# Four window products in adjoining slots: a denser slot table in the attention stage of a decoder layer

## The chip, the cores and the metric

The kernel runs on one core of one Trainium2 chip. The metric is the device time of one execution in microseconds. The engines are TensorE (PE: matmuls and transposes; its weight loads are listed apart as PEld), VectorE (DVE), ScalarE (ACT), GpSimd (POOL) and SyncE (SP), which here only issues DMAs. Each has its own in-order queue of instructions, and they meet at semaphores.

## The reference, cut to what matters

One layer of a decoder is computed for a prompt of 1024 tokens and for 8 samples of 4 new tokens each. The change touches the attention alone:

```python
DIL_CONFIGS = ((128, 1), (512, 4), (2048, 16))     # window, dilation; 8 heads x 64
# prompt: three dilated branches over its own k, v, combined by their softmax denominators
# sample: the same over the cached window (2048 rows of k and v) and the new rows
kc = jnp.concatenate([win_k, k], axis=1)
vc = jnp.concatenate([win_v, v], axis=1)
for _, dil in DIL_CONFIGS:
    o_i, l_i = dilated_branch_sample(q, kc, vc, dil)
attn = combine_branches(outs, lses)
```

Then follow a depthwise convolution module beside it, an output projection, cross-attention into 256 memory tokens and a gated FFN. The outputs are the new activations and the caches.

## The kernel before, in words

The three branches are one softmax with a bias that counts how many branches see a key. Of a sample's 2048 cached rows only 896 are seen by any branch: the last 512, and four in every sixteen of the older ones. Such a **window** is 7 tiles of 128 rows by 512 columns (1.8 MB), loaded by 4 DMAs (`window`, from L452). There are 16 of them, a key and a value window for each of 8 samples. They alternate between two buffers, `cached[0]` and `cached[1]`, in the order of `ORDER_W`: keys of samples 0 to 3, values of 0 to 3, keys of 4 to 7, values of 4 to 7. SP issues a window when the last reader of the one two places before it is done (L466 to L472); for a value window that reader is a **window product** (semaphore `spv`).

The stage is a loop over 34 **steps** (L1269). A prompt step s is one block i of 128 queries and one pair of heads. PE does, in step s: the scores of s (`scores`, in two parts from block 4 on), the product of probabilities and values of step s-2 (`product`), and the transposes of the probabilities of s-1 (`turn_p`, also in two parts). DVE adds the bias and takes the maxima (`maxima`, `negate`), ACT exponentiates (`probabilities`) and copies the transposes to SBUF (`turned`, tile `PT`).

The samples' attention is threaded through this loop in **slots**, three to a step from step 2 on. Slot number `r` of group `g` comes from `sample_slot` (L329): `divmod(3 * (s - 2) + pos, SAMPLE)`. There are two groups of four samples. In a group:

- slots 0 to 27: PE turns one key tile (`key_turn`), ACT or DVE copies it to `KTS` (ACT where the tile's number is divisible by 3, `on_scalar`), and in the next slot PE multiplies it with the queries (`key_scores`);
- slot 28 closes the scores; 29 and 30: bias and maximum on DVE, exponential on ACT; 32: normalisation of `Ps` on DVE; 33: PE transposes `Ps` (`turn_ps`); 34: ACT and DVE copy it to `PTS`;
- slots 35, 37, 39 and 41: the four window products (`window_product`), each 32 matmuls; slots 36, 38 and 40 are empty;
- slot 42: ACT copies the result to `OSs`; 43: PE turns it, and DVE copies it to `attsT`.

The order within a step is written out on each engine (L1269 to L1282 for PE, L1786 to L1799 for DVE, L674 to L688 for ACT). In PE's, the first slot stands behind the prompt product, the second behind the second part of the scores, the third at the end.

After the stage SP waits for the last prompt product (L474) and loads the memory rows (`mtk`), on whose norms PE's next matmuls depend.

Of the kernel before, what the change touches and what calls it, by code (L numbers as in the profile page):

```python
# [84 lines left out]
def pieces(c):  # L85

    out, g = [], c * CW
    while g < (c + 1) * CW:
        r = g % P
        n = min(P - r, (c + 1) * CW - g, (SEQ if g < SEQ else NTOK) - g)  # L90
        out.append((g // P, r, n, g - c * CW))
        g += n
    return out
# [11 lines left out]
class Signals:  # L105
# [14 lines left out]
    def mark(self, name, key, by=1):  # L120
        n = SHARED.get(name, name)
        self.now[n] = self.now.get(n, 0) + by
        assert (name, key) not in self.noted, (name, key)
        self.noted[name, key] = self.now[n]
        return self.sem(name), by
# [5 lines left out]
def layout(nc, ctx, A, O, counts):  # L131
# [183 lines left out]
    STEPS = [(i, hp) for i in range(TT) for hp in range(AT)]  # L315
    NP = len(STEPS)
    GROUP = 4 * KTILES
    SAMPLE = 44
    ORDER_W = [(kind, b) for g in range(2) for kind in "kv" for b in range(4 * g, 4 * g + 4)]
    STEP_W0 = 2  # L320
    LAST_STEP = max(NP + 1, STEP_W0 + 2 * SAMPLE // 3)

# [6 lines left out]
    def sample_slot(s, pos):  # L329
        g, r = divmod(3 * (s - STEP_W0) + pos, SAMPLE)  # L330
        return (g, r) if s >= STEP_W0 and g < 2 else (0, -1)

    def window_of(kind, b):
        n = ORDER_W.index((kind, b))
        return n, n % 2

    def on_scalar(n):
        return n % 3 == 0
# [211 lines left out]
    def _(act):  # L550
# [81 lines left out]
        def sample(g, r):  # L632

            if 0 <= r < GROUP and on_scalar(g * GROUP + r):
                n = g * GROUP + r
                act.wait_ge(*at("ktr", n))
                if n >= 2:
                    act.wait_ge(*at("ssc", n - 2))
                act.activation(KTS[n % 2][:, :, :], bank[5][:, :].rearrange("p (k n) -> p k n", k=AT), ACT.Copy).then_inc(*mark("ktsa", n))  # L639
            if r == GROUP + 2:  # L640
                act.wait_ge(*at("smax", g))
                act.activation(Ps[:, :], Ps[:, :], ACT.Exp, bias=negm[:, 2:3], accum_out=den[:, 2:3]).then_inc(*mark("sexp", g))
            if r == GROUP + 6:
                act.wait_ge(*at("sptr", g))
                if g:
                    act.wait_ge(*at("spv", 3))
                act.activation(PTS[:, 4:7, :], bank[7][:, 0:384].rearrange("p (a n) -> p a n", n=P), ACT.Copy).then_inc(*mark("spta", (g, 0)))
                act.activation(PTS[0:NS, KTILES, :], bank[7][0:NS, 384:512], ACT.Copy).then_inc(*mark("spta", (g, 1)))
            if r == GROUP + 14:
                act.wait_ge(*at("spv", 4 * g + 3))  # L650
                if g:
                    act.wait_ge(*at("sot", 0))
                else:
                    act.wait_ge(*at("cst_out", BD - 1))
                act.activation(OSs[:, :], bank[5][:, :], ACT.Copy).then_inc(*mark("os", g))
# [232 lines left out]
        for t in range(NX):  # L888
# [3 lines left out]
            g, even = divmod(t - HEAD0 - 1, 2)  # L892
# [144 lines left out]
        for g in range(2 * len(pieces(CH - 1))):  # L1037
            i, r, n, off = pieces(CH - 1)[g // 2]
# [16 lines left out]
    def _(pe):  # L1055
        reader = {}

        def take(b, name, key):

            if b in reader:  # L1060
                pe.wait_ge(*at(*reader[b]))
            reader[b] = (name, key)

        def turn(out, in_, r=0):
            n = in_.shape[0]
            return pe.transpose(out, in_, ident[r:r + n, r:r + n])  # L1066

        def mm(out, lhsT, rhs, first, last):
            return pe.matmul(out, lhsT, rhs, start=first, stop=last)  # L1069
# [162 lines left out]
        def window_product(b):  # L1232
            w, c = window_of("v", b)
            g = b // 4
            if b % 4 == 0:
                take(5, "os", g)
                pe.wait_ge(*at("spt", g))
                pe.wait_ge(*at("spta", (g, 1)))
            pe.wait_ge(*at(f"cached{c}", (w, OLD // P - 1)))
            cols = slice(P * (b % 4), P * (b % 4) + P)  # L1240
            for a in range(KTILES):
                for k in range(AT):
                    mm(bank[5][32 * k:32 * k + 32, cols], PTS[:, a, 32 * k:32 * k + 32], cached[c][:, a, k * P:(k + 1) * P], a == 0, False)
            for k in range(AT):
                ins = mm(bank[5][32 * k:32 * k + 32, cols], PTS[0:NS, KTILES, 32 * k:32 * k + 32], V[0:NS, TT, k * P:(k + 1) * P], False, True)
            ins.then_inc(*mark("spv", b))

        def sample(g, r):

            if r == 0:  # L1250
                group_scores(g)
            if 1 <= r <= GROUP:
                key_scores(g * GROUP + r - 1)
            if 0 <= r < GROUP:
                key_turn(g * GROUP + r)
            if r == GROUP:
                group_close(g)
            if r == GROUP + 5:
                turn_ps(g)
            if r - GROUP - 7 in (0, 2, 4, 6):  # L1260
                window_product(4 * g + (r - GROUP - 7) // 2)
            if r == GROUP + 15:
                take(5, "satt", (g, 3, 1))
                pe.wait_ge(*at("os", g))
                for b in range(4):
                    ins = turn(bank[5][:, b * P:(b + 1) * P], OSs[:, b * P:(b + 1) * P])
                ins.then_inc(*mark("sot", g))
# [320 lines left out]
        for g in range(2 * len(pieces(c))):  # L1588
            i, r, n, off = pieces(c)[g // 2]
# [8 lines left out]
    def _(dve):  # L1598
# [115 lines left out]
        def sample(g, r):  # L1714

            if 0 <= r < GROUP and not on_scalar(g * GROUP + r):
                n = g * GROUP + r
                dve.wait_ge(*at("ktr", n))
                if n >= 2:
                    dve.wait_ge(*at("ssc", n - 2))  # L1720
                dve.tensor_copy(KTS[n % 2][:, :, :], bank[5][:, :].rearrange("p (k n) -> p k n", k=AT)).then_inc(*mark("ktsd", n))
            if r == GROUP + 1:
                dve.wait_ge(*at("sall", g))
                if g:
                    dve.wait_ge(*at("sptr", g - 1))
                pieces_s = ((0, 512, bank[6][:, 0:512], ws[:, 0:512]), (512, KEYS, bank[7][:, 0:KEYS - 512], ws[:, 512:KEYS]),
                            (KEYS, KEYS + NS, bank[7][:, KEYS - 512:KEYS - 512 + NS], ws[:, KEYS + g * NS:KEYS + (g + 1) * NS]))
                for k, (k0, k1, src, bias) in enumerate(pieces_s):
                    if k:
                        dve.wait_ge(*at("sm", (g, k - 1)))  # L1730
                    masked_max(Ps[:, k0:k1], src, bias, mx[:, 0, k:k + 1], mx[:, 0, k - 1:k] if k else -3e38).then_inc(*mark("sm", (g, k)))
                dve.wait_ge(*at("sm", (g, 2)))
                dve.tensor_scalar(negm[:, 2:3], mx[:, 0, 2:3], -1.0, None, ALU.mult).then_inc(*mark("smax", g))
            if r == GROUP + 4:
                dve.wait_ge(*at("sexp", g))
                dve.reciprocal(rden[:, 2:3], den[:, 2:3]).then_inc(*mark("srd", g))
                dve.wait_ge(*at("srd", g))
                dve.tensor_scalar(Ps[:, :], Ps[:, :], rden[:, 2:3], None, ALU.mult).then_inc(*mark("spn", g))
            if r == GROUP + 6:
                dve.wait_ge(*at("sptr", g))  # L1740
                if g:
                    dve.wait_ge(*at("spv", 3))
                dve.tensor_copy(PTS[:, 0:4, :], bank[6][:, :].rearrange("p (a n) -> p a n", n=P)).then_inc(*mark("spt", g))
            if r == GROUP + 15:
                dve.wait_ge(*at("sot", g))
                for b in range(4):
                    v = bank[5][:, b * P:(b + 1) * P].rearrange("p (k y) -> p k y", y=32)
                    cols = slice((4 * g + b) * TD, (4 * g + b + 1) * TD)
                    for e in range(2):
                        rows = slice(64 * e, 64 * e + 64)  # L1750
                        dve.tensor_copy(attsT[rows, :, cols], v[rows, :, 8 * b + 4 * e:8 * b + 4 * e + 4]).then_inc(*mark("satt", (g, b, e)))
# [211 lines left out]
        for t in range(NX):  # L1963
            name, c, m = XU[t]
            g, odd = divmod(t - HEAD0 - 1, 2)
# [38 lines left out]
            g, odd = divmod(t - HEAD0, 2)  # L2004
# [78 lines left out]
        for g in range(2 * len(pieces(CH - 1))):  # L2083
            i, r, n, off = pieces(CH - 1)[g // 2]
# [42 lines left out]
```

## Time and profile before

| | |
|---|---|
| median of 3 runs | 1959.87 us (1957.81 to 1961.22) |
| the profiled execution | 1957.81 us, span 1955.7 us |
| PE busy | 1803.6 us, 92% of the span |
| DVE, ACT, POOL busy | 1018.8, 873.7, 834.1 us |
| mean granted clock of PE | 0.972 |
| DMA | 231.66 MB, mean 118 GB/s |

Busy time counts an engine's own work, not its waits. The span is that of the profiled core; the time of an execution is 2.1 us more. The attention stage reaches from about 316 to 569 us of the span.

### The profile page before, as it was taken

To read this page: it belongs to the slowest core of one execution; us is meant where nothing else is said; L and a number is where in the kernel's file an instruction comes from. 1 tells how busy PE (TensorE), PEld (TensorE's weight loads), DVE (VectorE), ACT (ScalarE), POOL (GpSimd) and SP (SyncE) were. 2 spreads that over 40 slices of the span, in tenths; PEclk is the share of its full clock that TensorE was granted. 3 is DMA by queue.
4 is the path that set the end of the run, shared out by engine and by line. 5 is a ranking of instruction groups with operands and counts; after the bars stand their busy time and mean duration, and the time that the engine had idled before them with its cause. 6 is when DMAs were issued, how large, how long until landed. Compare 5 with 4: busy or idle time off the path is not lost.

```text
span 1955.7 us, 30930 instructions
## 1 busy us (share of the span) xinstructions
PE 1803.6 (92%) x12222; PEld 1658.7 (85%) x12222; DVE 1018.8 (52%) x1749; ACT 873.7 (45%) x1663; POOL 834.1 (43%) x634
## 2 busy tenths in 40 slices
PE   3998997899968888789999988999999999999999
PEld 1898996567656778789887888999999999999998
DVE  3399992444425325773233567763148540388701
ACT  5211222344454545555544554554454543555533
POOL 1122231000002534454332445776667666677664
PEclk9999998999988889899999988999999999999999
DMA  5011223443212444444435333444444544444543
GB/s 170 22 46 41 88 82 115 140 163 114 80 57 65 121 135 124 116 142 154 129 115 171 93 93 101 140 133 137 134 137 140 151 143 137 138 138 140 150 135 105
DMA packets 348645, 231.66 MB, mean 118 GB/s; under 512 B 7915, under 2 KB 322401, under 8 KB 348495
## 3 DMA queue, kind: packets, MB, share of 16 engines
q1 hardware_dynamic: 342483, 218.19, 37.1%
q10 hardware_dynamic: 6020, 11.51, 1.6%
q8 instruction: 98, 1.61, 0.4%
q14 instruction: 44, 0.36, 0.1%
HBM read 218.58 MB, written 11.50 MB: 118 GB/s over the span
## 4 chain that ended last, share of the span: by engine, by line
PE 75%; DVE 14%; ACT 6%; issue 3%; DMA 2%; SPq 0%; ACTq 0%; POOL 0%; DVEq 0%
PE bank L1069 68%; PE bank L1066 7%; DVE C L1600 4%; DVE Y L1600 2%; DVE op_lo L1600 2%; DVE XT L1885 1%; DVE Sx L1873 1%; ACT whi L559 1%; ACT junk L572 1%; DVE cv L1600 1%; DVE carry L2043 1%; DVE Sy L1866 0%; SPq L413 0%; DVE op_x L1888 0%; ACT KTS L639 0%
## 5 line engine op out<-in xcount | busy, mean ns | idle before, releaser
L546 POOL TENSOR_TENSOR wlo<-raw,whi 128x512 fp32r<-128x512 f32 (+1 forms) x624 | 833.3, 1357 | 1103.3 <-ACT whi L559 1102.9
L1069 PE MATMUL bank<-op_hi,whi 128*128 128x352 f32 x1632 | 542.9, 333 | 10.2 <-ACT Y L810 8.7
L1069 PE MATMUL bank<-op_hi,wlo 128*128 128x352 f32 x1632 | 529.0, 324 | 0.0
L1069 PE MATMUL bank<-op_lo,whi 128*128 128x352 f32 x1632 | 528.3, 324 | 0.0
L559 ACT ACTIVATE whi<-raw 128x1024 fp32r<-128x1024 f32 (+1 forms) x312 | 325.1, 1043 | 303.8 <-PE bank L1069 84.2
L1069 PEld LDWEIGHTS bank<-op_hi,whi 128*128 128x128 f32 x1632 | 310.5, 190 | 20.0 <-ACT Y L810 9.9
L1069 PEld LDWEIGHTS bank<-op_lo,whi 128*128 128x128 f32 x1632 | 311.6, 191 | 0.3
L1069 PEld LDWEIGHTS bank<-op_hi,wlo 128*128 128x128 f32 x1632 | 310.1, 190 | 0.0
L1866 DVE TENSOR_TENSOR Sy<-Sy,SQy 128x352 f32<-128x352 f32 x63 | 40.2, 638 | 297.9 <-ACT SQy L772 297.9
L1600 DVE SCALAR_TENSOR_TENSOR C<-U,cw,C 128x1024 f32<-128x1024 f32 x120 | 176.5, 1471 | 4.0
L1069 PE MATMUL bank<-fhi,whi 128*128 128x352 f32 x528 | 171.1, 324 | 0.0
L1069 PE MATMUL bank<-fhi,wlo 128*128 128x352 f32 x528 | 170.8, 323 | 0.0
L1069 PE MATMUL bank<-h1hi,whi 128*128 128x352 f32 x480 | 157.6, 328 | 5.8 <-DVE U L1680 5.8
L1069 PE MATMUL bank<-h1lo,whi 128*128 128x352 f32 x480 | 155.6, 324 | 0.0
L1069 PE MATMUL bank<-h1hi,wlo 128*128 128x352 f32 x480 | 155.3, 324 | 0.0
L1600 DVE SCALAR_TENSOR_TENSOR cv<-aext,fw,cv 128x352 f32<-128x352 f32 (+2 forms) x176 | 109.6, 654 | 63.5 <-ACT aext L982 42.2
L1069 PEld LDWEIGHTS bank<-fhi,wlo 128*128 128x128 f32 x528 | 99.8, 189 | 0.0
L1069 PEld LDWEIGHTS bank<-fhi,whi 128*128 128x128 f32 x528 | 99.3, 188 | 0.0
L1069 PEld LDWEIGHTS bank<-h1hi,whi 128*128 128x128 f32 x480 | 91.5, 191 | 6.4 <-DVE U L1680 6.3
L1069 PEld LDWEIGHTS bank<-h1lo,whi 128*128 128x128 f32 x480 | 91.6, 191 | 0.0
L1069 PEld LDWEIGHTS bank<-h1hi,wlo 128*128 128x128 f32 x480 | 91.4, 190 | 0.0
L1069 PEld LDWEIGHTS bank<-V,PT 128*128 128x128 f32 x576 | 67.1, 192 | 22.0 <-issue 21.1
(274 smaller groups left out, 2631.8 us busy)
## 6 DMA issues: line engine op xcount, KB each, us to landing
raw<-in_w_up_dram SPq DMA_DIRECT2D x132, 512.0 KB, 3.8
raw<-in_w_down_dram SPq DMA_DIRECT2D x48, 512.0 KB, 3.8
raw<-in_w_out_dram SPq DMA_DIRECT2D x24, 512.0 KB, 3.8
raw<-in_w_xq_dram SPq DMA_DIRECT2D x24, 512.0 KB, 3.9
raw<-in_w_xo_dram SPq DMA_DIRECT2D x24, 512.0 KB, 3.8
raw<-in_w_in_dram SPq DMA_DIRECT2D x20, 512.0 KB, 3.7
raw<-in_w_down_dram SPq DMA_DIRECT2D x24, 384.0 KB, 3.3
cached<-in_cache_win_k_dram SPq DMA_DIRECT2D x8, 1024.0 KB, 5.8
```

The source lines that it names most:

```text
L546: pool.tensor_tensor(wlo[u % SLOTS][:, ks, :], raw[u % SLOTS][:, ks, :], whi[u % SLOTS][:, ks, :].bitcast(F32), ALU.subtract).then_inc(*ma ...
L559: act.activation(whi[v % SLOTS][:, 0:nk, :], raw[v % SLOTS][:, 0:nk, :], ACT.Copy).then_inc(*mark("w_hi", v))
L572: act.activation(junk[0:n, :], xt[i][0:n, hf * 512:(hf + 1) * 512], ACT.Square, accum_out=ssx[0:n, i, hf:hf + 1]).then_inc(*mark("xss", (i ...
L1066: return pe.transpose(out, in_, ident[r:r + n, r:r + n])
L1069: return pe.matmul(out, lhsT, rhs, start=first, stop=last)
L1600: return dve.scalar_tensor_tensor(out=out, in0=in0, scalar=scalar, in1=in1, op0=op0, op1=op1)
L1866: dve.tensor_tensor(Sy[:, :], Sy[:, :], SQy[:, :], ALU.add).then_inc(*mark("ysum", (name, c, m)))
L1873: dve.tensor_tensor(Sx[:, :], Sx[:, :], SQx[m % 2][:, :], ALU.add).then_inc(*mark("xsum", (name, c, m)))
L1885: dve.tensor_tensor(XT[c][:, m, :], XT[c][:, m, :], y[:, m, :], ALU.add).then_inc(*mark(*key))
L2043: ins = dve.tensor_copy(carry[:, :, j], a[:, n:n + 2])
```

## The change

The slots of a group become 42 instead of 44. The four window products stand in slots 35, 36, 37 and 38. The copy to `OSs` moves from slot 42 to 39, and turning it from 43 to 40; slot 41 is empty. Group 1 starts two slots earlier, in the first slot of step 16 instead of the third. `LAST_STEP` stays 33.

```diff
-    SAMPLE = 44
+    SAMPLE = 42
@@ ACT, sample(g, r)
-            if r == GROUP + 14:
+            if r == GROUP + 11:
                 act.wait_ge(*at("spv", 4 * g + 3))
@@ PE, sample(g, r)
-            if r - GROUP - 7 in (0, 2, 4, 6):
-                window_product(4 * g + (r - GROUP - 7) // 2)
-            if r == GROUP + 15:
+            if 0 <= r - GROUP - 7 < 4:
+                window_product(4 * g + r - GROUP - 7)
+            if r == GROUP + 12:
                 take(5, "satt", (g, 3, 1))
@@ DVE, sample(g, r)
-            if r == GROUP + 15:
+            if r == GROUP + 12:
                 dve.wait_ge(*at("sot", g))
```

On PE, group 0, from window product 1 on (`cached_107` and `cached_108` are the two buffers, `Pp` the prompt's probabilities) the order before is:

```order
L1069 MATMUL bank<-cached_108,PTS 32x128 [waits cached1]
L1069 MATMUL bank<-cached_108,PTS 32x128 x27
L1069 MATMUL bank<-V,PTS 32x128 x4
L1069 MATMUL bank<-KT,QT 128x512 [waits pmax] x2
L1069 MATMUL bank<-V,PT 128x128 [waits pt,att]
L1069 MATMUL bank<-V,PT 128x128 x3
L1069 MATMUL bank<-V,PT 128x128 [waits pt]
L1069 MATMUL bank<-V,PT 128x128 x3
L1069 MATMUL bank<-cached_107,PTS 32x128 [waits cached0]
```

And in the changed kernel, from the same window product 1 on:

```order
L1069 MATMUL bank<-cached_108,PTS 32x128 [waits cached1]
L1069 MATMUL bank<-cached_108,PTS 32x128 x27
L1069 MATMUL bank<-V,PTS 32x128 x4
L1066 MATMUL bank<-ident,Pp_111 128x128 [waits pt,pexp]
L1066 MATMUL bank<-ident,Pp_111 128x128 x3
L1066 MATMUL bank<-ident,Pp_111 128x128 [waits pt,pexp]
L1066 MATMUL bank<-ident,Pp_111 128x128 x3
L1069 MATMUL bank<-cached_107,PTS 32x128 [waits cached0]
L1069 MATMUL bank<-cached_107,PTS 32x128 x27
L1069 MATMUL bank<-V,PTS 32x128 x4
L1069 MATMUL bank<-cached_108,PTS 32x128 [waits cached1]
```

Between products 1 and 2 stood the scores and the prompt product of the next step; now 8 transposes stand there, and product 3 follows product 2 at once.

On ACT, the copies of group 1's key tiles to `KTS` in step 17 (L670 copies prompt transposes, L662 exponentiates) stood between the two parts of the prompt's copies:

```order
L670 ACTIVATE PT<-bank 128x512 [waits pv,ptr] x2
L639 ACTIVATE KTS_113<-bank 128x512 [waits ssc,ktr]
L670 ACTIVATE PT<-bank 128x128 [waits pv,ptr] x2
L662 ACTIVATE Pp_111,pden<-Pp_111,pneg 128x640 [waits pmax] x2
L670 ACTIVATE PT<-bank 128x512 [waits pv,ptr] x2
```

In the changed kernel they stand behind the exponentials:

```order
L662 ACTIVATE Pp_110,pden<-Pp_110,pneg 128x640 [waits pmax] x2
L639 ACTIVATE KTS_113<-bank 128x512 [waits ssc,ktr]
L670 ACTIVATE PT<-bank 128x512 [waits pv,ptr] x2
L670 ACTIVATE PT<-bank 128x128 [waits pv,ptr] x2
L662 ACTIVATE Pp_111,pden<-Pp_111,pneg 128x640 [waits pmax] x2
```

ACT's tiles moved from the second to the third slot of a step. The tile turned in the second slot is now one of DVE's, where it stands behind the second part of the maxima (L1604) and the negation (L1771):

```order
L1604 ISA Pp_111,pmx<-bank,wt,pmx 128x128 [waits pmax,ptr,score]
L1604 ISA pmx 128x1
L1771 TENSOR_SCALAR pneg<-pmx 128x2 [waits pmax]
L1721 COPY KTS_113<-bank 128x512 [waits ssc,ktr]
L1604 ISA Pp_110,pmx<-bank,wt 128x512 [waits ptr,score]
```

These are DVE's rows of the changed kernel around the end of step 17. The orders of SP and POOL are the same in both kernels.

## Rows read from the trace of the kernel before

**Rows 1.** The page, part 4: the chain of work that ended last, by engine.

```profile
PE 75%; DVE 14%; ACT 6%; issue 3%; DMA 2%; SPq 0%; ACTq 0%; POOL 0%; DVEq 0%
```

**Rows 2.** PE's waits, 388 to 570 us: us in total, times, longest.

```profile
PE bank L1069 <- ACT KTS L639: 2.9, 8, 0.5
PE bank L1069 <- DMA cached<-in_cache_win_v_dram: 1.6, 1, 1.6
PE bank L1069 <- ACT PTS L648: 1.5, 1, 1.5
PE bank L1066 <- DVE Ps L1738: 1.5, 1, 1.5
```

**Rows 3.** Timeline of PE, steps 13 to 15: start, us, line, tiles, count, [idle before].

```profile
397.48 1.74 PE L1069 MATMUL bank<-cached,PTS 128*32 128x128 f32 x56 [1.45 <-ACT PTS L648]
...
399.50 1.13 PE L1069 MATMUL bank<-KT,QT 64*128 64x512 f32 x4
...
402.44 1.04 PE L1066 MATMUL bank<-ident,Pp 128*128 128x128 f32 x8
403.41 1.74 PE L1069 MATMUL bank<-cached,PTS 128*32 128x128 f32 x56
...
405.43 1.13 PE L1069 MATMUL bank<-KT,QT 64*128 64x512 f32 x4
...
413.16 1.74 PE L1069 MATMUL bank<-cached,PTS 128*32 128x128 f32 x56 [1.58 <-DMA cached<-in_cache_win_v_dram]
```

**Rows 4.** Timeline of SP's queue, the issues of value windows 2 and 3.

```profile
399.63 2.37 SPq L413 DMA_DIRECT2D cached<-in_cache_win_v_dram  x4
...
405.56 2.48 SPq L413 DMA_DIRECT2D cached<-in_cache_win_v_dram  x4
```

**Rows 5.** Stretches: length, busy us of PE, PEld, DVE, ACT, POOL; PEclk, DMA share, GB/s.

```profile
406.50:407.00 0.50, 0.50 (x6) 0.50 (x5) 0.41 (x1) 0.00 (x0) 0.00 (x0) 1.00 0.42 111
...
412.50:413.00 0.50, 0.00 (x0) 0.00 (x0) 0.00 (x0) 0.50 (x3) 0.00 (x0) 1.00 0.29 90
```

**Rows 6.** Timeline of PE, two key tiles, in steps 8 and 17.

```profile
366.74 0.66 PE L1066 MATMUL bank<-ident,cached 128*128 128x128 f32 x4
368.18 0.43 PE L1069 MATMUL bank<-KTS,QW 128*32 128x128 f32 x8 [0.78 <-DVE KTS L1721]
...
428.23 0.66 PE L1066 MATMUL bank<-ident,cached 128*128 128x128 f32 x4
...
429.57 0.43 PE L1069 MATMUL bank<-KTS,QW 128*32 128x128 f32 x8 [0.47 <-ACT KTS L639]
```

**Rows 7.** Timeline of PE and DVE, step 24: key turning and negation.

```profile
489.41 0.66 PE L1066 MATMUL bank<-ident,cached 128*128 128x128 f32 x4
...
490.36 0.17 DVE L1771 TENSOR_SCALAR pneg<-pmx 128x2 f32<-128x2 f32 x1
```

**Rows 8.** SP's issues of value windows 6 and 7, and a stretch after them.

```profile
528.33 2.37 SPq L413 DMA_DIRECT2D cached<-in_cache_win_v_dram  x4
...
535.53 2.44 SPq L413 DMA_DIRECT2D cached<-in_cache_win_v_dram  x4
...
542.50:543.00 0.50, 0.50 (x7) 0.50 (x6) 0.50 (x2) 0.00 (x0) 0.00 (x0) 1.00 0.00 0
```

**Rows 9.** SP's issue of the memory rows, at the stage's end.

```profile
569.28 0.82 SPq L413 DMA_DIRECT2D mtk<-in_mem_prompt_dram  x2
```

**Rows 10.** Stretches around a change of clock; prompt products at either clock.

```profile
319.20:328.90 9.70, 6.37 (x30) 3.30 (x34) 3.56 (x29) 2.08 (x10) 0.00 (x0) 0.50 0.95 364
...
641.00:643.20 2.20, 0.27 (x3) 0.02 (x1) 0.42 (x1) 2.20 (x5) 1.95 (x2) 1.00 0.43 125
643.30:646.00 2.70, 1.33 (x3) 0.86 (x4) 0.00 (x0) 1.61 (x4) 2.05 (x2) 0.50 0.31 94
...
325.06 1.19 PE L1069 MATMUL bank<-V,PT 128*128 128x128 f32 x4 [1.86 <-ACT PT L670]
...
333.92 0.71 PE L1069 MATMUL bank<-V,PT 128*128 128x128 f32 x4
```

## The prediction

> **What bounds the kernel now.** I read the chain of waits first: three quarters of it is TensorE (PE), and DMA is 2% [rows 1]. So a change pays or costs what it does to PE's idle time. The change acts only in the attention stage (about 316 to 569 us of the span), so I read the list of PE's waits there next, from 388 to 570 us [rows 2]. PE waits very little: 2.9 us in 8 waits for ScalarE's (ACT) copy of a turned key tile, 1.6 us once for a value window, 1.5 us once for the copy of the turned sample probabilities (PTS) and 1.5 us once for their normalisation (Ps). Almost all the rest is PE at work, and the change removes no instruction. All it can win are these four numbers, 7.5 us together; what it can lose has no such limit. PE's queue is in order: a wait in a sample slot holds back the prompt's scores behind it, and with them VectorE (DVE) and ACT.
>
> **Part 1: the value products of group 0.** Windows alternate between two buffers, so window v2 is issued by SP when product 0 is done, and v3 when product 1 is done. Before [rows 3]: product 0 runs 397.48 to 399.50, then step 14 does scores and the prompt's product (399.50 to 402.44, 2.94 us), its transposes (to 403.41, 0.97 us) and product 1 (2.02 us, to 405.43). Step 15 holds products 2 and 3; product 3 waits 1.58 us and starts at 413.16. SP issues v2 at 399.63 and v3 at 405.56 [rows 4], each 0.13 us after the product that frees the buffer. The data of v2 run out between 406.5 and 407.0 and those of v3 between 412.5 and 413.0 [rows 5]; product 3's start at 413.16 dates the landing of v3 at 7.6 us after its issue, and v2's is about 7.2 us, at 406.9.
>
> Now all four products stand in slots 35 to 38: product 0 at the end of step 13 as before, and 1, 2 and 3 in step 14. Product 1 runs 402.44 to 404.46, transposes to 405.43, product 2 waits for v2 to 406.9 (1.45 us) and ends at 408.9. v3 is issued at 404.6 while v2 still moves; its landing is at 411.7 (7.1 us later, no delay) to 412.7 (held back by the 1 us in which both are under way). I take 412.0, near the rows. Product 3 waits 3.1 us and ends at 414.0. Step 15 then has only scores, prompt product and transposes left, 2.94 + 0.97 us, and step 16 begins at 417.9. Before, with the same work done, it began at 413.16 + 2.02 = 415.2. **Cost 2.7 us**, bounds 2.3 and 4.2.
>
> **Part 2: the key tiles of group 1.** Group 1 now begins in the first slot of step 16, not the third. That moves every key tile by one place in a step, and ACT serves each third tile by its number. Between second and third slot PE has almost nothing (the short second transposes), so it waits for the copy. Before, this copy was ACT's: from one key turning to the next scores 428.23 to 429.57, 1.34 us. Now it is DVE's; group 0 shows that case, 366.74 to 368.18, 1.44 us [rows 6]. Moreover, in these steps DVE has first to do the second part of the maxima and the negation. At 384 columns the negation starts at 490.36, 0.95 us after the key turning at 489.41, and DVE is free 0.1 us later [rows 7]; the turned tile is ready 0.70 us after its turning begins (group 0's 1.44 us less its copy of about 0.7). So +0.35 us on top there. At 128 columns DVE is free before the tile is, at 256 about 0.1 us late. Nine pairs: 9 x 0.1, plus 4 x 0.1, plus 0.35 = **1.6 us**. The last pair was in step 25, where the wait hid 6 transposes (6/8 of the 0.97 us that eight take in rows 3, 0.7 us); it goes to step 16, which has no second transposes. **0.7 us** more. Bounds 0.5 (only the engine's difference, half hidden) and 3.5.
>
> **Part 3: softmax of group 1.** Group 1 gets the slot-in-step positions that group 0 has. PE no longer waits for Ps (1.5 us), since scores and product now stand between, but it meets group 0's wait for PTS (1.5 us) [rows 2]. **Net nothing**, bounds -1.5 and +1.
>
> **Part 4: the value products of group 1.** Now product 4 stands in step 27, and 5, 6 and 7 in step 28. A window lands 7.0 us after its issue here: v7, issued at 535.53, has no traffic left after 542.5 [rows 8]; with the 0.13 us before the issue, 7.1 us after the product that frees the buffer. Between the ends of products 4 and 5 stand scores (1.06 us, the 1.13 us of rows 3 without the overlap), a prompt product of 28 matmuls (against 16 in step 14, which took 1.9 us, so 3.3 us) and product 5 itself (2.02); transposes (0.97) and second scores (1.06) follow. That is 8.4 us, so product 6 does not wait. Between product 5 and product 7 there are only transposes 0.97, scores 1.06, product 6 2.02 and 6 transposes 0.7, together 4.75 us. **A new wait of 2.4 us**, where before four slots lay between their starts and there was none. Bounds 1.5 and 3.5.
>
> Nothing hides the sum: the memory rows are issued right after the last prompt product, at 569.28 [rows 9], and PE then idles until they are through, so a later end of the stage passes on in full. The two saved slots held no PE instruction; they only moved where prompt and sample work meet. Sum: 2.7 + 1.6 + 0.7 + 0 + 2.4 = **7.4 us**.
>
> **The clock.** PE's granted clock is one of two levels, 2.4 GHz (1.00) and 1.2 GHz (0.50). From 641 to 643.2 us PE was busy 0.27 of 2.2 us at 1.00, and the next stretch, from 643.3, shows 0.50. Four matmuls of a prompt product took 1.19 us at 325.06, in a stretch at 0.50, against 0.71 us at 333.92, so work is up to 1.7 times as long [rows 10]. The three waits of 1.5 us in the stage left the clock up. The new pair in step 14 idles PE 4.5 of 6.6 us with only product 2 between; I expect a fall there. If 3 to 4 us of work (product 3 and the start of step 15) run slow it costs 1.2 to 1.7 us; I take 1.5. The 2.4 us wait in step 28 may cause another.
> The Trainium skill ("TensorE: Matmul & The Clock Gate", section "HAM oscillation — how this bites in real kernels") describes this pattern: about 2 us of matmuls between DMA waits, each wait dropping the clock so that the next tile starts cold. [...]
>
> **Rivals.**
> 1. Waits and one fall (forecast): 7.4 + 1.5 = 8.9 us. The profiled execution took 1957.81 us (span 1955.7), so 1966.7 there; on the median of the runs, 1959.87, **1968.8**. Chance 0.35.
> 2. Waits and a fall in each place: the wait in step 28 is long enough too, and the last product and the start of step 29 run at 0.50, another 1.5 us: +10.4, 1970.3. Chance 0.20. [...]
> 3. Waits, no fall: +7.4, 1967.3. For it: the clock survived product 3's wait before. Chance 0.20.
> 4. Low clock that persists in both places over several steps: with 6 to 8 us more at 1.7 times, +7.4 + 2 x 3 = +13.4, 1973.3. Chance 0.10.
> 5. The waits are mostly made good: parts 2 and 4 hidden, part 1 alone, about +2.5, 1962.4. Against it: PE has no idle time there to give back. Chance 0.11.
> 6. Faster. The windows come in time, no new wait, and the earlier group takes the old ones away: 1.6 + 1.5 + 1.5 = 4.6 us gained, 1955.3. Place: products 2 and 3 of step 14. It decides at a landing 5.8 us after the issue for v2 (by 405.43) and 2.85 us for v3 (by 407.45). Rows 3 to 5 show over 7. Chance 0.04.
> That the change does nothing is excluded: the order of PE, DVE and ACT moves.
>
> **How the numbers follow.** About 0.2% (3.9 us) is what a measurement here tells from no change. Slower by more: cases 1 to 4 (0.85) and 0.01 of case 5, 0.86. Within it: the rest of case 5, 0.10. Faster: case 6, 0.04. The range reaches from case 5, whose lower half stays out, past case 4: 1962.5 to 1974. Case 1 with the bounds of its parts gives 1965 to 1972.
>
> **What would show it.** PE's waits for the value windows should be three, near 1.5, 3.1 and 2.4 us; those for key tiles move from ACT to DVE and grow from 2.9 to about 4.5 us; the wait for Ps gone and one for PTS twice; the stage's end (memory rows issued) 7 to 10 us after 569.28; a stretch at 0.50 after about 411 us. If windows land in under 3 us, or the end of the stage doesn't move, the argument is wrong.

## The result, and the profile after

The changed kernel takes 1975.64 us, median of 6 runs (1973.04 to 1977.58), against 1959.53 us for the kernel before in the same comparison (6 runs, 1957.18 to 1961.22). The ratio is 1.0083, 95% interval 1.0069 to 1.0096: 16.1 us slower, where 8.9 were forecast. The whole interval lies above no change, and the time just above the forecast's range of 1962.5 to 1974. The profiled execution took 1973.56 us, span 1971.6 us.

PE's waits in the stage, after (us in total, times, longest), to be held against [rows 2]:

```profile
PE bank L1069 <- DMA cached<-in_cache_win_v_dram: 9.2, 3, 5.2
PE bank L1069 <- DVE KTS L1721: 5.2, 9, 0.8
PE bank L1069 <- ACT PTS L648: 1.5, 1, 1.5
PE bank L1069 <- issue: 1.3, 1, 1.3
```

The value windows' waits grew from 1.6 to 9.2 us and are three. Those for key tiles moved from ACT to DVE and grew from 2.9 to 5.2. The wait for Ps is gone, and a wait of 1.3 us stands before product 4 (the line with "issue"). It ends when DVE's copy to PTS is through, at 529.77; this copy came behind the second maxima and the negation:

```profile
529.08 0.69 DVE L1743 COPY PTS<-bank 128x512 f32<-128x512 f32 x1
529.87 1.74 PE L1069 MATMUL bank<-cached,PTS 128*32 128x128 f32 x56 [1.29 <-issue]
```

Now PE's timeline in step 14 and what follows, against [rows 3]:

```profile
403.97 1.74 PE L1069 MATMUL bank<-cached,PTS 128*32 128x128 f32 x56
...
408.68 1.74 PE L1069 MATMUL bank<-cached,PTS 128*32 128x128 f32 x56 [1.59 <-DMA cached<-in_cache_win_v_dram]
...
416.00 3.21 PE L1069 MATMUL bank<-cached,PTS 128*32 128x128 f32 x56 [5.24 <-DMA cached<-in_cache_win_v_dram]
419.14 0.57 PE L1069 MATMUL bank<-V,PTS 32*32 32x128 f32 x8
419.65 1.13 PE L1069 MATMUL bank<-KT,QT 64*128 64x512 f32 x4
```

Product 3 waits 5.24 us, and then takes from 416.00 to 419.65, 3.65 us instead of 2.0: the same 56 records last 3.21 us instead of 1.74. SP's queue shows the issues, against [rows 4]:

```profile
401.06 2.32 SPq L413 DMA_DIRECT2D cached<-in_cache_win_v_dram  x4
406.12 2.90 SPq L413 DMA_DIRECT2D cached<-in_cache_win_v_dram  x4
```

Window v2 lands 7.6 us after its issue (401.06 to 408.68), v3 9.9 us after (406.12 to 416.00). In group 1 it is product 7 that waits, for window v7, issued 6.4 us behind v6:

```profile
532.01 2.39 SPq L413 DMA_DIRECT2D cached<-in_cache_win_v_dram  x4
538.41 3.02 SPq L413 DMA_DIRECT2D cached<-in_cache_win_v_dram  x4
545.61 3.08 PE L1069 MATMUL bank<-cached,PTS 128*32 128x128 f32 x56 [2.35 <-DMA cached<-in_cache_win_v_dram]
```

The stretches around both waits (length, busy us of PE, PEld, DVE, ACT, POOL, then PEclk, DMA share, GB/s), to be held against [rows 5, 10]:

```profile
408.50:412.50 4.00, 2.09 (x64) 1.62 (x64) 0.00 (x0) 0.67 (x2) 0.00 (x0) 1.00 0.90 288
412.80:419.40 6.60, 3.40 (x64) 2.76 (x64) 0.00 (x0) 0.00 (x0) 0.00 (x0) 0.50 0.94 335
...
542.50:545.70 3.20, 0.85 (x10) 0.61 (x14) 0.00 (x0) 2.73 (x5) 0.00 (x0) 1.00 0.76 287
545.90:549.10 3.20, 3.20 (x64) 2.53 (x52) 0.00 (x0) 0.19 (x2) 0.00 (x0) 0.50 0.02 5
```

The clock fell to 1.2 GHz at 412.7, within the wait for v3, and at 545.8, at the end of the wait for v7. PE had been idle half of the 4 us before 412.5 and three quarters of the 3.2 us before 545.7. Products 3 and 7 ran at the low clock; the scores behind each took 1.13 us again, as in [rows 3]. The end of the stage, where [rows 9] showed 569.28:

```profile
583.95 0.82 SPq L413 DMA_DIRECT2D mtk<-in_mem_prompt_dram  x2
```

I measure the stage from the scores of step 13 (391.56 before, 393.00 after) to this issue: 177.72 us before, 190.95 after, **13.2 us more**. It splits as follows.

| part of the stage | forecast | measured |
|---|---|---|
| waits for v2 and v3 (1.59 + 5.24, less 1.58 before) | 2.7 | 5.25 |
| product 3 at the low clock (3.65, less 2.02) | 1.5 | 1.6 |
| key tiles, softmax of group 1 (steps 16 to 27, up to product 4) | 2.3 | 1.7 |
| wait for v7 | 2.4 | 2.35 |
| product 7 at the low clock (3.59, less 2.02) | 0 (a rival's) | 1.6 |
| the last steps, without sample work in them | 0 | 0.75 |
| sum | 8.9 | 13.25 |

The spans of the two profiles differ by 15.9 us. The other 2.7 us lie before the scores of step 13 (1.44) and after the stage (1.23).

### The profile page after: what moved, and what is told of

Same layout as the page of the kernel before. It is cut to its first block, busy times and chain, and to the rows that moved or that the text cites. A ratio compares the mean times of both kernels' runs of the same rounds, so it can differ in the third digit from the quotient of the medians.

```text
span 1971.6 us, 30930 instructions
## 1 busy us (share of the span) xinstructions
PE 1809.5 (92%) x12222; PEld 1664.1 (84%) x12222; DVE 1019.3 (52%) x1749; ACT 874.4 (44%) x1663; POOL 836.0 (42%) x634
## 4 chain that ended last, share of the span: by engine, by line
PE 77%; DVE 12%; ACT 5%; issue 3%; DMA 2%; SPq 1%; ACTq 0%; DVEq 0%
PE bank L1069 70%; PE bank L1066 7%; DVE C L1600 4%; DVE Y L1600 2%; DVE op_lo L1600 1%; DVE XT L1885 1%; DVE Sx L1873 1%; ACT whi L559 1%; ACT junk L572 1%; DMA cached<-in_cache_win_v_dram 1%; DVE KTS L1721 1%; SPq L413 1%; DVE cv L1600 0%; DVE Sy L1866 0%; DMA out_dram<-MKO 0%
```

## The experiments

All times are medians, beside runs of the kernel before on the same chip; "stage" is the length defined above, in the run's profile.

**Only the adjoining products.** 44 slots, so that group 1 begins where it did.

```diff
-    SAMPLE = 42
+    SAMPLE = 44
```

> Products in adjoining slots 35 to 38 as in the changed kernel, but 44 slots to a group, so group 1 begins where it did before. Theory W (landing waits of the value windows and the clock falls behind them carry the loss): group 0 loses as in the changed kernel (waits 1.6 and 5.2 us, a fall of the clock), about +6.9 us; in group 1 products 4, 5 are in step 28 and 6, 7 in step 29, with the scores and a prompt product of step 29 between 5 and 6, so 7.1 us pass before 6 and over 8 before 7: no wait there. Key copies stay with ACT (2.9 us of waits). Total about +7, 1966.5. Theory S (the shift of group 1 by two slots carries the loss: other engine for the key copies, bare last steps): at most +4, below 1963.6.

Measured: 1967.12 us, ratio 1.0050 (1.0033 to 1.0066), stage 186.63, 8.9 us more than before. Group 0 lost 6.6 us. In group 1 there were two small waits, where I had expected none:

```profile
543.21 1.74 PE L1069 MATMUL bank<-cached,PTS 128*32 128x128 f32 x56 [1.45 <-DMA cached<-in_cache_win_v_dram]
...
547.78 1.74 PE L1069 MATMUL bank<-cached,PTS 128*32 128x128 f32 x56 [0.40 <-DMA cached<-in_cache_win_v_dram]
```

Theory W stands, and the adjoining products alone make the kernel slower. The clock fell twice in group 0 here, and products 2 and 3 both ran at 1.2 GHz. The rest of the 8.9 us are the two small waits and 0.56 us of longer scores in a late step, which come back below. v6 came 8.6 us after product 4's end (534.6), not 7.1, with v7 issued 2.8 us behind it. So a window issued closely behind can delay the one in front.

**Only the shift.** The kernel before with one slot more to a group, which puts group 1 into the slots of a step that the change gives it.

```diff
-    SAMPLE = 44
+    SAMPLE = 45
```

> The kernel before with 45 slots to a group: products spaced as before, group 1 one slot later, so its slots stand where the changed kernel has them within a step, one step later. Theory W: one landing wait of 1.6 us as before; key copies on DVE, 5.2 us of waits instead of 2.9; the wait for Ps gone and one for PTS in its place. Total +2 to +2.5 us, about 1961.8. Theory S: +6 or more, 1965.5 or above.

Measured: 1958.25 us, ratio 0.9993 (0.9981 to 1.0005), stage 179.52, 1.8 us more. PE's waits for DVE's key copies are 5.0 us in 9 times, one of 1.6 us stands before product 4, the one for Ps is gone. The stage answers to theory W, and theory S falls. The time does not show the 1.8 us (the interval ends at +1.0): in this profile the part after the stage was 5.6 us shorter than before. PE's mean granted clock was 0.975 or 0.976 in 8 of these 10 executions, and 0.970 to 0.974 in 25 of the 26 of the kernel before beside them. The expected 1961.8 was missed. That the shift does not carry the loss is shown, its exact price in the time is not.

**No landing waits.** The changed kernel without value windows 2, 3, 6 and 7, and the kernel before likewise. The edit, in both:

```diff
-    ORDER_W = [... for b in range(4 * g, 4 * g + 4)]
+    ORDER_W = [... for b in range(4 * g, 4 * g + (4 if kind == "k" else 2))]
-        n = ORDER_W.index((kind, b))
+        n = ORDER_W.index((kind, b if kind == "k" else b - b % 4 + b % 2))
-        for n in range(2, 2 * BD):
+        for n in range(2, len(ORDER_W)):
-                sp.wait_ge(*at("spv", b))
+                sp.wait_ge(*at("spv", b + 2))
```

> The changed kernel, but value windows 2, 3, 6 and 7 are not loaded: products 2, 3, 6 and 7 read windows 0, 1, 4 and 5 again, so 4 of 16 windows (7.3 MB) are left out, and the sample outputs of these samples are computed from the wrong values. Theory W: the waits of 1.6, 5.2 and 2.35 us vanish, and with them both falls of the clock (1.6 us each): 12.4 us less than the changed kernel, 1963.2. Theory S: the loss lies in the shift; PE meets other waits and the time stays at 1969 or above.

> The kernel before with the same four value windows left out, as a control for the traffic taken away. Both theories: only the 1.6 us landing wait of product 3 goes, 1958.0; were it 4 us or more below the kernel before, traffic itself costs time here and the run beside it (the changed kernel with these windows left out) must be read against this one.

Measured: the changed kernel 1959.76 us, ratio 0.9999 (0.9988 to 1.0010), stage 178.35; the kernel before 1957.00, ratio 0.9995 (0.9984 to 1.0005), stage 176.06. Between the two stages lie 2.3 us, where 13.2 lay with the windows loaded. So 10.9 of the 13.2 us come from the landings and what follows them: the waits (9.2 less 1.6) and the two slow products (3.2) make 10.8. In the changed kernel's stage without them no stretch at 1.2 GHz is left.

**What delays v3: the key window behind it?**

```diff
-                sp.wait_ge(*at("spv", b))
+                sp.wait_ge(*at("spv", 3 if n == 8 else b))
```

> The changed kernel, but SP issues key window 4 when product 3 is done, not when product 2 is. Value window 3 landed 9.9 us after its issue in the changed kernel, against 7.6 before. Theory K (key window 4, issued 4.7 us behind it, shares the DMA engines with its tail; about 0.3 MB of it moved before the landing): product 3's wait falls from 5.2 to about 4.3 us and the time by 1 us. Theory V (window 3 is slowed by being queued behind window 2, which is still in flight): the landing stays within 0.3 us of 9.9 and the wait at 5.0 or more. Both: nothing in group 1 changes unless key window 4 comes too late, which would show as a wait of PE for win_k.

Measured: 1972.91 us, ratio 1.0072 (1.0055 to 1.0089), stage 191.15. PE and SP in that kernel:

```profile
407.18 2.99 PE L1069 MATMUL bank<-cached,PTS 128*32 128x128 f32 x56 [1.63 <-DMA cached<-in_cache_win_v_dram]
414.59 3.21 PE L1069 MATMUL bank<-cached,PTS 128*32 128x128 f32 x56 [3.84 <-DMA cached<-in_cache_win_v_dram]
```

```profile
404.59 3.14 SPq L413 DMA_DIRECT2D cached<-in_cache_win_v_dram  x4
...
418.21 3.05 SPq L413 DMA_DIRECT2D cached<-in_cache_win_k_dram  x5
```

The key window was issued at 418.2, after v3 had landed, and v3 still took 10.0 us (404.59 to 414.59). Theory K is out. With no other window behind it, the end of v3 can be seen by itself. For the last 2.5 us before 414.0 PE has nothing to do and the DMA engines are busy for 0.37 of the time (the column before GB/s):

```profile
409.00:411.50 2.50, 1.75 (x32) 0.91 (x24) 0.00 (x0) 0.00 (x0) 0.00 (x0) 0.62 0.92 319
411.50:414.00 2.50, 0.00 (x0) 0.00 (x0) 0.00 (x0) 0.00 (x0) 0.00 (x0) 1.00 0.37 143
```

So the last part of v3 moves at less than half the flow, 143 GB/s against 319. The wait is shorter here (3.84) only because product 2 itself ran at the low clock and filled part of it: the landing is what is fixed, not the wait. My expectation of 5.0 or more for the wait missed that.

**Or the window in front of it?** SP issues v3 when v2 has landed.

```diff
+            if n == 7:
+                sp.wait_ge(*at("cached0", (6, OLD // P - 1)))
             window(n)
```

> The changed kernel, but SP issues value window 3 only when window 2 has landed, instead of 2.6 us before that. Theory G (a window issued behind one in flight gains nothing: its 6 us of data begin when the other's end, and its flow is thinner): window 3 lands 7.2 to 7.6 us after the landing of window 2, product 3 waits 5.0 to 5.7 us, and the stage is as long as in the changed kernel within 0.5 us. Rival Q (queueing ahead hides the 1.1 us between an issue and the first data, and window 3 was held up by something else): product 3 waits 6.3 us or more and the stage is 1.1 us or more longer.

Measured: 1974.72 us, ratio 1.0083 (1.0060 to 1.0106), stage 191.01, the changed kernel's within 0.1 us. PE and SP (the two added lines move line numbers by 2):

```profile
406.83 1.74 PE L1071 MATMUL bank<-cached,PTS 128*32 128x128 f32 x56 [1.43 <-DMA cached<-in_cache_win_v_dram]
414.54 3.18 PE L1071 MATMUL bank<-cached,PTS 128*32 128x128 f32 x56 [5.62 <-DMA cached<-in_cache_win_v_dram]
```

```profile
399.39 2.41 SPq L413 DMA_DIRECT2D cached<-in_cache_win_v_dram  x4
406.85 2.42 SPq L413 DMA_DIRECT2D cached<-in_cache_win_v_dram  x4
```

v3 is issued 2.4 us later than it could be and lands at the same place: product 3 begins 23.2 us after the scores of step 13, and 23.0 us in the changed kernel. It lands 7.7 us after its own issue and 7.7 us after v2, 0.1 us more than theory G's 7.2 to 7.6. Theory G holds for this load: the head start of v3, some 2.5 us, is lost in full.

It is no general rule, and the kernel before shows both cases. There v3 is issued 5.9 us behind v2 and 1.7 us before v2's landing, and keeps that head start: it lands 7.6 us after its issue ([rows 3, 4]). Key window 4, for which PE does not wait, is issued 5.1 us behind v3 at 410.62 and lands at 420.9, 10.3 us later. The times from issue to landing of the 4 DMAs of one window, for v3 before, key window 4 before and v3 after:

```profile
DMA to landing us min/median/max: 5.3/5.6/5.7
...
DMA to landing us min/median/max: 6.2/7.2/8.6
...
DMA to landing us min/median/max: 5.4/6.7/8.2
```

v7 of the changed kernel, 6.4 us behind v6 and 1.1 us before its landing, lands 7.2 us after its issue. Why a head start of 1 to 1.7 us is kept and one of 2.5 us lost, I can't say.

**ACT for the second slot's key tile**, in the changed kernel.

```diff
-        return n % 3 == 0
+        return n % 3 == (0 if n < GROUP else 2)
```

> The changed kernel, but in group 1 ACT copies the key tiles turned in the second slot of a step, as before the change (rule: tile number mod 3 is 2 instead of 0). My theory of part 2: PE's waits for key copies fall from 5.2 us by the engine's and DVE's share, 1.6 us, to about 3.6 (0.7 of what is left above the 2.9 of before is the pair that moved from step 25 to 16), and the stage ends 1.6 us earlier. Rival: the copy's place, not the engine, sets the wait, and it stays near 5.

Measured: 1974.29 us, ratio 1.0077 (1.0062 to 1.0092), stage 190.03. PE's waits:

```profile
PE bank L1069 <- DMA cached<-in_cache_win_v_dram: 10.0, 3, 5.6
PE bank L1069 <- ACT KTS L639: 3.6, 9, 0.7
```

The key waits fell from 5.2 to the 3.6 us expected. The stage gained only 0.9 us, since the windows' waits were 0.8 us longer in this execution. The waits bear out part 2 of the forecast, in mechanism and size; the time, 1974.29 against 1975.64 us, cannot tell.

**The price of the clock.** Matmuls without use fill PE's two long waits; first 40 and 18 of them, then 20 and 8.

```diff
+            for _ in range({3: 20, 7: 8}.get(b, 0)):
+                mm(bank[6][:, 0:P], ident[:, :], KT[:, 0, 0:P], True, True)
             pe.wait_ge(*at(f"cached{c}", (w, OLD // P - 1)))
```

> The changed kernel with matmuls without use in PE's two long waits: 40 of 128 columns (4.6 us) before product 3 and 18 (2.1 us) before product 7, into a bank that is free there. Theory C (the two falls of the clock behind these waits cost about 1.6 us each): no stretch at 1.2 GHz in the stage, products 3 and 7 take 2.0 us instead of 3.65 and 3.6, and the stage ends 3.2 us earlier, 1972.4. Rival: the falls cost nothing, or the added matmuls run past the landing: the end of the stage stays or moves later by up to 1 us.

Measured with 40 and 18: 1976.58 us, ratio 1.0085 (1.0068 to 1.0102), stage 193.67. The matmuls take 0.23 us each (9.20 us for 40), twice what I had counted, since each leaves two records in the profile. They ran past the landing: product 3 began at 419.90. The clock stayed up, but the run doesn't tell the price. So again with half:

> The changed kernel with matmuls without use in PE's two long waits, this time short enough to end before the landings: 20 matmuls (0.23 us each as measured with 40, so 4.6 us) before product 3 and 8 (1.8 us) before product 7. Theory C (each fall of the clock behind these waits costs 1.6 us): no stretch at 1.2 GHz between steps 14 and 29, products 3 and 7 take 2.0 us, the stage ends 3.2 us earlier than in the changed kernel (from the scores of step 13 to the issue of the memory rows 187.8 us instead of 190.95), time 1972.4 or with the downward part of its noise 1970. Rival: the falls are not worth more than 0.5 us each and the stage stays at 190 or above.

Measured: 1969.95 us, ratio 1.0054 (1.0033 to 1.0075), stage 188.42, against 190.95: 2.5 us less, where 3.2 were expected. PE there:

```profile
409.41 4.73 PE L1069 MATMUL bank<-KT,ident 128*128 128x128 f32 x40
414.83 1.74 PE L1069 MATMUL bank<-cached,PTS 128*32 128x128 f32 x56 [0.69 <-DMA cached<-in_cache_win_v_dram]
...
543.43 1.74 PE L1069 MATMUL bank<-cached,PTS 128*32 128x128 f32 x56 [1.16 <-DMA cached<-in_cache_win_v_dram]
```

Both products take 1.74 us for their 56 records again, at 1.00. v3 landed 9.9 us after its issue, as in the changed kernel; v7 landed 0.6 us later after its issue than in the changed kernel, which takes most of the missing 0.7 us. The falls are real and cost about 1.3 us each by the stage, 1.6 by the products' own rows. More work on PE made the stage shorter. The time points the same way (the changed kernel, run beside it once more, took 1973.51 us), but the two intervals of the ratio overlap.

**The other direction.** The kernel before with the products in slots 36, 38, 40 and 42.

```diff
-            if r - GROUP - 7 in (0, 2, 4, 6):
-                window_product(4 * g + (r - GROUP - 7) // 2)
+            if r - GROUP - 8 in (0, 2, 4, 6):
+                window_product(4 * g + (r - GROUP - 8) // 2)
```

> The kernel before (44 slots) with the four products in slots 36, 38, 40 and 42 instead of 35, 37, 39 and 41: the other direction. If PE's waits are what counts: the PTS wait of group 0 (1.5 us) goes, since scores and a prompt product stand before product 0; product 3 finds its window 8.9 us after product 1 and waits no more (1.6 us); product 2 may wait 0.2 us. The stage ends 2.8 us earlier, 1957. Rival (the places of sample work within the last steps matter as much): product 6 and 7 both in step 30 change nothing or cost 1 to 2 us, and the time is 1959 to 1960.

Measured: 1959.00 us, ratio 0.9993 (0.9982 to 1.0004), stage 177.05, 0.7 us less than before and not the 2.8 expected. PE's waits:

```profile
PE bank L1066 <- DVE Ps L1738: 1.5, 1, 1.5
PE bank L1069 <- DMA cached<-in_cache_win_v_dram: 1.4, 1, 1.4
PE bank L1066 <- DMA cached<-in_cache_win_k_dram: 1.1, 1, 1.1
```

The wait for PTS in group 0 is gone and so is product 3's, but product 2 now waits 1.4 us and the first key tile of group 1 waits 1.1. Windows are in flight together again: v2, with v3 issued 3.0 us behind it, lands 8.2 us after its issue, and key window 4, issued 2.4 us before v3's landing, 9.7 us after its own. No version that beats the kernel before by a measurable amount came out.

**Both kernels once more.**

> The changed kernel once more, for a second profile: the stage explained 13.2 of 16.1 us. If the other 2.9 us are chance (the clock's falls after the stage, the start of the program), the stage repeats within 0.5 us of 190.95 and the parts before and after it differ from the first profile by up to 3 us either way, and overlap with those of the kernel before. If the changed kernel makes the work after the stage slower, its part after the stage stays above all of those of the kernel before.

> The kernel before once more, for a second profile beside that of the changed kernel. The stage, from the scores of step 13 to the issue of the memory rows, repeats within 0.5 us of 177.72; the part after the stage (1386.4 in the first profile) tells how much it varies by itself.

Measured: the changed kernel 1973.51 us, ratio 1.0078 (1.0062 to 1.0094), stage 190.93; the kernel before, a single run, 1958.59 us, stage 177.44. The stages repeat within 0.3 us, so the 13.2 us are firm (13.5 in this pair). The split within group 0 does not repeat. In the second profile the clock fell already at 407.7, behind the wait for v2:

```profile
407.29 2.85 PE L1069 MATMUL bank<-cached,PTS 128*32 128x128 f32 x56 [1.50 <-DMA cached<-in_cache_win_v_dram]
...
414.72 3.21 PE L1069 MATMUL bank<-cached,PTS 128*32 128x128 f32 x56 [4.01 <-DMA cached<-in_cache_win_v_dram]
```

Product 2 ran slowly and product 3 waited 4.0 us instead of 5.2, for the same landing (9.9 us after the issue). That fall cost nothing in the stage, since the longer product 2 came out of the wait for v3. The part after the stage was 1387.65 and 1389.57 us in the changed kernel, and 1386.4 and 1386.8 before. That is 1 to 3 us more, on the one side of my condition, but the other variants spread from 1380.8 to 1389.1. Whether the change costs anything there is open.

## Why the prediction was wrong, point by point

- **What bounds the stage** was right: PE and its waits, and none of the later stage end was made good behind it (the part after the stage was 1.2 us longer, not shorter).
- **Part 1, the landing of v3, is the step that failed.** I put it 7.1 us after its issue plus up to 1 us for the window in front, and took 412.0, a wait of 3.1 us; the bound was 412.7. What came was the landing of v2 plus nearly a whole window, 406.9 + 7.5 = 414.4 on the forecast's scale, a wait of 5.5; 5.24 was measured. Two runs show it: without a head start v3 lands at the same place, and moving the key window behind it changes nothing. The waits for v2 and v3 cost 5.25 us where the forecast had 2.7, and its bounds ended at 4.2. The rows that I quoted could not show it, since v3 was issued 5.9 us behind v2 there. The trace could: key window 4, 5.1 us behind v3, took 10.3 us. I also read v2's landing from the end of its traffic, as 406.9; the trace has its last DMA landing at 407.3. Why the distance of 5.1 us costs the whole head start stays open.
- **The clock.** One fall of 1.5 us was the forecast, a fall in each place the rival with 0.20; the rival came, at 1.6 us each. That is the second term missed. The Trainium skill ("TensorE: Matmul & The Clock Gate", section "HAM oscillation — how this bites in real kernels") describes matmuls of about 2 us between waits for DMA of 3 to 5 us, each tile starting cold. This case agrees, with products of 3.65 and 3.59 us against 2.0, and the second came behind a shorter wait, of 2.35 us. The forecast's remark that waits of 1.5 us left the clock up is true of the kernel before and no rule: in the repeat of the changed kernel the clock fell behind one of 1.50 us.
- **Part 2** was right: 5.2 us of waits against 2.9, with the moved pair in it, and the engine change undone takes 1.6 us off the waits. **Part 3** was right in size: Ps 1.5 us gone, 1.3 us before product 4 in its place. The copy waited for is DVE's, not ACT's as in group 0. Together they came 0.6 us cheaper than I summed.
- **Part 4** was right to 0.1 us: a wait of 2.35. v7 was issued 1.1 us before v6 landed and still came 7.2 us after its own issue, so the failed step didn't matter there.
- **Not foreseen: 0.75 us in the last steps.** In step 31 the scores take 0.56 us longer than in [rows 3]:

```profile
564.87 1.69 PE L1069 MATMUL bank<-KT,QT 64*128 64x512 f32 x4
```

and DVE is still at the maxima of step 30's second part, whose bank these scores need:

```profile
564.63 0.75 DVE L1604 CUSTOM_DVE_ANT_0 Pp<-bank,wt,pmx 128x512 f32<-128x512 f32 x1
```

  It ends at 565.38. In the kernel before, product 7 stood between step 30's second scores and these, in the second slot of step 30, and gave DVE the time. Every profile without a product at this place has 1.68 or 1.69 us in step 31, the run with adjoining products and 44 slots among them; the others have 1.13. Step 30's first scores take 1.25 us, another 0.12.
- **The sum.** The stage lost 4.35 us more than forecast: 2.55 in part 1, 1.6 for the second fall, 0.75 in the last steps and 0.1 for the first fall, less 0.6 in parts 2 and 3 and 0.05 in part 4. The memory rows were issued 14.7 us after 569.28, where 7 to 10 were forecast; 1.44 of these lay before the stage. 13.2 of the 16.1 us are in the stage. The second comparison gave 13.8 us. What lies between is within the two intervals, and I don't assign it.
- **The other rivals.** "Faster" needed v2 within 5.8 us and v3 within 2.85 us of their issues; 7.6 and 9.9 were measured. "Made good" fails at the stage's end, which moved by the whole sum. A low clock over several steps did not come: both stretches ended with the product.

## What to carry to other kernels

An empty slot between two users of a double buffer is not idle time if a load is under way in it. Before closing it, write down for each load when it is issued, what is in flight then, and when it lands, and give a load behind another two bounds: its own issue plus the time of a load alone, and the landing of the other plus that time. Here a head start of up to 1.7 us was kept, with one exception, and one of about 2.5 us was lost. Where a wait of 2 to 5 us then appears on PE, add the slower work behind it. Where an engine is always busy, a shorter slot table takes nothing off; only its waits can be shortened.

## What the runs showed of the hardware

- v2, a window of 1.8 MB in 4 DMAs, landed 7.4 to 7.7 us after its issue in all profiles in which no window was in flight then and none was issued within 5 us behind it. v3 issued 5.1 us behind it landed after 9.6 to 10.2 us; issued when v2 had landed, after 7.7 us, at the same place; issued 5.9 us behind it (the kernel before, twice, and the shifted one), after 7.3 to 7.6 us. v7 issued 6.4 us behind v6 landed after 7.2 to 7.8 us in six profiles and after 9.1 us in one (with 40 and 18 matmuls without use).
- What PE did before each fall to 1.2 GHz in this stage: in the changed kernel it waited 1.59 us, ran product 2 and waited 5.24 us (fall at 412.7), and it waited 2.35 us before product 7 (fall at 545.8). In the repeat it waited 1.50 us (fall at 407.7), ran product 2 and waited 4.01 us (fall at 414.6). In the kernel before, with single waits of 1.5 and 1.6 us, no fall stands in the stage. Matmuls without use in both waits kept the clock up.
- A matmul of 128 columns in fp32 took 0.23 us at 2.4 GHz (9.20 us for 40).
